# Hybrid encoder block on one Trainium2 core: a new order of the beginning (norm gains spread by TensorE, weight split shared by two engines, idle TensorE fed transposes)

## The chip, the cores and the metric

The kernel runs on one core of one Trainium2 chip. The metric is the time of one execution in device microseconds, the median of three runs. Times of single instructions come from one profiled execution. Engines are named as the profile names them: PE is TensorE, DVE is VectorE, ACT is ScalarE, POOL is GpSimd, SP issues the DMAs.

## The reference, cut to what matters

One layer, 1024 tokens of width 1024, all in float32:

```
h    = rmsnorm(x, norm_mix)                  # x * rsqrt(mean(x*x) + eps) * norm_mix
proj = h @ w_in                              # 2208 columns, split in
qa, ka, va, ga, cq, ckv, kr, gb              # 512,128,128,512,384,256,32,512
ya = window_attention(qa, ka, va) * silu(ga)
q  = rmsnorm(cq, q_a_norm) @ w_uq            # latent attention
kv = rmsnorm(ckv, kv_a_norm) @ w_ukv
yb = latent_attention(q, kv, rope(kr)) * silu(gb)
out = rmsnorm(x + concat(ya, yb) @ w_out, final_norm)
```

The change touches only the start: `h`, and the "natural" part of the projection, the 800 columns `va`, `cq`, `ckv`, `kr`, which come out with the tokens on the partitions.

## The kernel before, in words

Every float32 product is made of three matmuls: each operand is split in a part `hi` rounded to the fp32r type and the rest `lo`, and `three()` adds hi*hi, hi*lo and lo*hi in PSUM (L1097 to L1101). There are eight blocks `k` of 128 weight rows (`KT`) and eight tiles `t` of 128 tokens (`NT`). Each engine runs its own instruction list strictly in the order in which the code issues it, and the engines meet only at semaphores, so the order around the change is written out by hand.

The path of one token tile at the start: SP loads `x_in` (512 KB, two buffers). ACT squares it and sums the row (`s_ssq`). DVE turns the sum into a variance (`s_var`), ACT takes the root (`s_rms`), DVE takes the reciprocal and multiplies x, the scale and the gains `g_mix` in one instruction (L831, `s_xn`). PE transposes the tile in eight pieces into PSUM banks 0 and 1 (`turn_x`, `s_xT`). ACT copies each bank to `hT_hi` (`h_hi`), DVE subtracts it to make `hT_lo` (`h_lo`, `s_hT`). The gains were loaded by a DMA that writes `norm_mix` to all 128 partitions.

The path of one weight block: SP loads 800 of its columns into one of three buffers `wn_raw`. POOL copies them to `wn_hi` (L406) and subtracts for `wn_lo` (L408), then signals `s_wnr`.

PE multiplies tile t with block k by `natural(t, c, ks)`, in two column groups c: 416 columns (va, ckv, kr) in one PSUM bank and 384 (cq) in another, three matmuls each. `nat_banks(t)` gives the banks of tile t; there are three pairs, so tile 3 takes those of tile 0. Tiles 0 to 2 are worked on together, block by block, as blocks come in; the transposes of tiles 3 to 7 are put between the blocks. From tile 3 on, PE does a whole tile at a time, and before each waits for `s_lat` of the tile three before it: ACT and DVE must have taken that tile out of its banks. They do this in the "lat loop" (L613 and L848), whose first step is tile 0 and which both engines enter only after the last `h_hi` and `h_lo`: a copy of va, two squares with sums, a copy of kr, a root, a reciprocal and two scaled writes of `lat` (L861, L864; `s_lat`). `lat` is then transposed (`turn_lat`). Behind this stage come the up-projections and the attention, in which PE goes on without long pauses.

Of the kernel before, what the change touches and what calls it, by code (L numbers as in the profile page):

```python
# [32 lines left out]
P = 128  # L33
# [26 lines left out]
NA = P + KVL + ROPE  # L60
NW = NA + QL

# [9 lines left out]
def encoder(nc, x, norm_mix, w_in, attn_sink, q_a_norm, w_uq, kv_a_norm, w_ukv, w_out, final_norm,  # L72
# [7 lines left out]
    with ExitStack() as ctx:  # L80
# [21 lines left out]
        g_lat = at("g_lat", 144.5, [P, QL + KVL])  # L102
        lat = at("lat", 147, [P, 2, QL + KVL])
# [62 lines left out]
        ssq, var, rms, rstd = (stat[:, 8 * i:8 * i + 8] for i in range(4))  # L166
        lss, lvar, lrms, lrstd = (stat[:, 32 + 2 * i:34 + 2 * i] for i in range(4))
# [20 lines left out]
        s_wnh, s_wnr = sem("wn_hi_ready"), sem("wn_ready")  # L188
        s_pA, s_pB = sem("natA_done"), sem("natB_done")
# [88 lines left out]
        def _(sp):  # L278
            def load_x(t):
                if t >= 2:  # L280
                    sp.wait_ge(s_xn, t - 1)
                sp.dma_start(x_in[:, t % 2, :], x[t * P:(t + 1) * P, :]).then_inc(s_x[t % 2], 16)

            def load_wn(k):
                if k >= 3:
                    sp.wait_ge(s_wnr, k - 2)
                rows = w_in[k * P:(k + 1) * P, :]
                sp.dma_start(wn_raw[:, k % 3, 0:P], rows[:, VA:VA + P]).then_inc(s_wn[k % 3], 16)
                sp.dma_start(wn_raw[:, k % 3, P:NA], rows[:, CKV:CKV + KVL + ROPE]).then_inc(s_wn[k % 3], 16)
                sp.dma_start(wn_raw[:, k % 3, NA:NW], rows[:, CQ:CQ + QL]).then_inc(s_wn[k % 3], 16)  # L290
# [15 lines left out]
            sp.wait_ge(s_wnr, KT)  # L306
# [96 lines left out]
        def _(pool):  # L403
# [176 lines left out]
        def _(act):  # L580
# [10 lines left out]
            for t in range(NT):  # L591
                if t == 3:
                    h_hi(t - 1)
# [19 lines left out]
            for t in range(NT):  # L613
                a, b = nat_banks(t)
                act.wait_ge(s_pA, t + 1)
                nc.scalar.activation(vA[:, t, :, 0:HD], ps[:, a, 0:P].rearrange("p (g c) -> p g c", c=HD),
                                     ACT.Copy)
                if t >= 2:
                    act.wait_ge(s_lT, t - 1)
                nc.scalar.activation(lat[:, t % 2, QL:QL + KVL], ps[:, a, P:P + KVL], ACT.Square,  # L620
                                     accum_out=lss[:, 1:2])
                nc.scalar.activation(kr_n[:, t, :], ps[:, a, P + KVL:NA], ACT.Copy).then_inc(s_va, 1)
                act.wait_ge(s_pB, t + 1)
                nc.scalar.activation(lat[:, t % 2, 0:QL], ps[:, b, 0:QL], ACT.Square,
                                     accum_out=lss[:, 0:1]).then_inc(s_lss, 1)
# [177 lines left out]
        def _(dve):  # L803
# [17 lines left out]
            for t in range(NT):  # L821
                if t == 3:
                    h_lo(t - 1)
                dve.wait_ge(s_ssq, t + 1)
                nc.vector.tensor_scalar(var[:, t:t + 1], ssq[:, t:t + 1], 1.0 / D, EPS, ALU.mult,
                                        ALU.add).then_inc(s_var, 1)
                dve.wait_ge(s_rms, t + 1)
                link(nc.vector.reciprocal(rstd[:, t:t + 1], rms[:, t:t + 1]))
                if t == 0:
                    dve.wait_ge(s_gmix, 16)  # L830
                nc.vector.scalar_tensor_tensor(out=x_n[:, t % 2, :], in0=x_in[:, t % 2, :],  # L831
                                               scalar=rstd[:, t:t + 1], in1=g_mix[:, :], op0=ALU.mult,
                                               op1=ALU.mult).then_inc(s_xn, 1)
                if t >= 1 and t != 3:
                    h_lo(t - 1)
# [12 lines left out]
            for t in range(NT):  # L848
# [247 lines left out]
        def _(pe):  # L1096
# [19 lines left out]
            def natural(t, c, ks):
# [3 lines left out]
                for k in ks:  # L1120
                    last = three(ps[:, nat_banks(t)[c], 0:w1 - w0], hT_hi[:, k, toks], hT_lo[:, k, toks],
# [14 lines left out]

            pe.wait_ge(s_id, 2)

            turn_x(0)
            turn_x(1)  # L1140
            for k in range(KT - 2):
                for t in range(3):
                    if k == 0:
                        pe.wait_ge(s_hT, 2 * (t + 1))
                    pe.wait_ge(s_wnr, k + 1)
                    for c in range(2):
                        natural(t, c, range(k, k + 1))
                    if k == 0 and t == 0:
                        turn_x(2)
                if k >= 1:  # L1150
                    turn_x(2 + k)
            pe.wait_ge(s_wnr, KT)
            for t in range(3):
                for c in range(2):
                    natural(t, c, range(KT - 2, KT))
# [256 lines left out]
```

## Time and profile before

| what | value |
|---|---|
| median of 3 runs | 655.42 us (654.73 to 655.53) |
| the profiled execution's own time | 655.55 us |
| its span in the trace | 653.8 us |
| PE busy | 632.7 us, 97% of the span |
| DVE, ACT, POOL busy | 407.8, 331.8, 302.1 us |

PE's busy time and the span differ by 21.1 us. The page's 40 slices are 16.3 us each: PE has a 3 in the first, a 6 in the last and 9 in all others, so the larger part of PE's idle time lies in the first 20 us.

### The profile page before, as it was taken

How to read it: one execution, taken by the hardware profiler on the slowest of the kernel's cores; microseconds unless marked ns; L12 is line 12 of the kernel's file. 1: busy time of each engine (PE TensorE's matmuls, PEld its weight loads, DVE VectorE, ACT ScalarE, POOL GpSimd, SP SyncE). 2: the span in 40 equal slices, each digit the busy share in tenths (PEclk: the TensorE clock that was granted, in tenths of full speed). 3: DMA queues.
4: the chain of work that ended last, by engine and by line, in shares of the span. 5: the costliest groups of instructions: out<-in, count | busy, mean ns of one | idle time of the engine just before them, and what ended most of it. 6: DMA issues, size and time to landing. Idle time of an engine off the chain costs nothing.

```text
span 653.8 us, 8923 instructions
## 1 busy us (share of the span) xinstructions
PE 632.7 (97%) x3252; PEld 536.6 (82%) x3252; DVE 407.8 (62%) x773; ACT 331.8 (51%) x717; POOL 302.1 (46%) x283
## 2 busy tenths in 40 slices
PE   3999999999999999999999999999999999999996
PEld 3899998888888878888878788888888887888884
DVE  4863326334221158999985988888888888955422
ACT  4542222213222147777774877777777778404312
POOL 4962004402323244363545776876786777820000
PEclk9999999999999999999999999999999999999998
DMA  7730006363121210100122101011013201403521
GB/s 238 232 123 0 1 29 240 142 250 101 34 65 33 64 34 1 32 2 1 48 99 73 40 2 42 12 30 41 1 42 102 100 1 34 161 1 125 181 81 65
DMA packets 31612, 47.38 MB, mean 72 GB/s; under 512 B 2544, under 2 KB 19440, under 8 KB 31440
## 3 DMA queue, kind: packets, MB, share of 16 engines
q1 hardware_dynamic: 31568, 46.81, 22.6%
q8 instruction: 26, 0.43, 0.3%
q14 instruction: 18, 0.15, 0.1%
HBM read 35.13 MB, written 11.67 MB: 72 GB/s over the span
## 4 chain that ended last, share of the span: by engine, by line
PE 91%; DVE 3%; ACT 2%; issue 1%; DMA 1%; POOL 1%; SPq 0%; ACTq 0%; DVEq 0%; POOLq 0%
PE ps L1099 21%; PE ps L1101 21%; PE ps L1100 21%; PE ps L1308 8%; PE ps L1324 4%; PE ps L1325 4%; PE ps L1241 2%; PE ps L1251 2%; PE ps L1252 1%; PE ps L1230 1%; PE ps L1229 1%; DMA g_mix<-norm_mix 1%; PE ps L1111 1%; PE ps L1133 1%; DVE x_n L831 1%
## 5 line engine op out<-in xcount | busy, mean ns | idle before, releaser
L523 POOL TENSOR_SCALAR p_b<-p_b,stat 128x1024 f32<-128x1024 f32 x64 | 71.9, 1123 | 52.9 <-DVE stat L1023 52.2
L738 ACT ACTIVATE pT_hi<-ps 128x512 fp32r<-128x512 f32 x128 | 69.9, 596 | 38.5 <-PE ps L1308 38.4
L1018 DVE TENSOR_REDUCE stat<-ps 128x1 f32<-128x1024 f32 x64 | 77.7, 1213 | 10.2 <-PE ps L1101 10.1
L1099 PE MATMUL ps<-hT_hi,w_hi 128*128 128x512 f32 x208 | 83.7, 402 | 0.0
L1028 DVE TENSOR_TENSOR pT_lo<-ps,pT_hi 128x512 fp32r<-128x512 f32 x128 | 81.8, 680 | 1.4 <-ACT pT_hi L738 1.4
L1101 PE MATMUL ps<-hT_hi,w_lo 128*128 128x512 f32 x208 | 81.3, 391 | 0.0
L1100 PE MATMUL ps<-hT_lo,w_hi 128*128 128x512 f32 x208 | 81.0, 390 | 0.0
L729 ACT ACTIVATE p_b<-ps,stat 128x1024 f32<-128x1024 f32 x64 | 71.5, 1118 | 12.0 <-DVE stat L1018 11.7
L1308 PEld LDWEIGHTS ps<-ident,p_b 128*128 128x128 f32 x512 | 59.3, 141 | 12.1 <-issue 2.6
L1308 PE MATMUL ps<-ident,p_b 128*128 128x128 f32 x512 | 67.3, 273 | 1.0 <-DVE pT_lo L1028 0.9
L406 POOL TENSOR_SCALAR w_hi<-w_raw 128x1024 fp32r<-128x1024 f32 x13 | 14.1, 1081 | 91.4 <-PE ps L1101 91.4
L466 POOL TENSOR_SCALAR p_w<-p_w,stat 128x384 f32<-128x384 f32 (+1 forms) x48 | 27.8, 596 | 60.1 <-DVE stat L949 60.1
L1324 PE MATMUL ps<-pT_hi,vB 128*128 128x512 f32 x128 | 55.3, 432 | 0.0
L1101 PE MATMUL ps<-k_hi,q_lo 96*128 96x512 f32 x128 | 50.5, 394 | 0.0
L1100 PE MATMUL ps<-k_lo,q_hi 96*128 96x512 f32 x128 | 50.5, 394 | 0.0
L1099 PE MATMUL ps<-k_hi,q_hi 96*128 96x512 f32 x128 | 50.3, 393 | 0.0
L1325 PE MATMUL ps<-pT_lo,vB 128*128 128x512 f32 x128 | 50.3, 393 | 0.0
L1101 PE MATMUL ps<-wo_hi,y_lo 128*128 128x512 f32 x128 | 49.8, 389 | 0.0
L1100 PE MATMUL ps<-wo_lo,y_hi 128*128 128x512 f32 x128 | 49.8, 389 | 0.0
L1099 PE MATMUL ps<-wo_hi,y_hi 128*128 128x512 f32 x128 | 49.8, 389 | 0.0
L1099 PE MATMUL ps<-wn_hi,hT_hi 128*128 128x384 f32 (+1 forms) x128 | 45.7, 357 | 0.4 <-DVE hT_lo L815 0.4
L1101 PEld LDWEIGHTS ps<-hT_hi,w_lo 128*128 128x128 f32 x208 | 39.0, 188 | 8.5
(155 smaller groups left out, 1433.1 us busy)
## 6 DMA issues: line engine op xcount, KB each, us to landing
w_raw<-w_in SPq DMA_DIRECT2D x13, 512.0 KB, 3.9
x_in<-x SPq DMA_DIRECT2D x8, 512.0 KB, 3.7
wo_raw<-w_out SPq DMA_DIRECT2D x8, 512.0 KB, 4.4
x_r<-x SPq DMA_DIRECT2D x8, 512.0 KB, 3.7
out<-o_n SPq DMA_DIRECT2D x16, 256.0 KB, 2.4
q_nope_scratch<-stage SPq DMA_DIRECT2D x8, 256.0 KB, 2.8
k_nope_scratch<-stage SPq DMA_DIRECT2D x8, 256.0 KB, 2.1
v_scratch<-stage SPq DMA_DIRECT2D x8, 256.0 KB, 2.0
```

What stands on the lines that cost most here:

```text
L466: nc.gpsimd.tensor_scalar(p_w[:, u % 2, r, 0:w], p_w[:, u % 2, r, 0:w], w_col(5, u)[:, r:r + 1], 0.5, ALU.mult, ALU.mult).then_inc(s_wp, 1)
L523: nc.gpsimd.tensor_scalar(p_b[:, (U + 1) % 4, :], p_b[:, (U + 1) % 4, :], r_b[:, U % 4:U % 4 + 1], 0.5, ALU.mult, ALU.mult).then_inc(s_bp, 1)
L729: nc.scalar.activation(p_b[:, (U + 1) % 4, :], ps[:, b:b + 2, :].rearrange("p b c -> p (b c)"), ACT.Exp, bias=nm_b[:, U % 4:U % 4 + 1], ac ...
L738: nc.scalar.activation(pT_hi[:, G % 2, 4 * a:4 * a + 4, U % 4 * P:(U % 4 + 1) * P], ps[:, 4 + a, :].rearrange("p (k c) -> p k c", c=P), AC ...
L1018: nc.vector.tensor_reduce(nm_b[:, U % 4:U % 4 + 1], ps[:, b:b + 2, :].rearrange("p b c -> p (b c)"), AX.X, ALU.max, negate=True).then_inc( ...
L1028: nc.vector.tensor_tensor(pT_lo[at_], ps[:, 4 + a, :].rearrange("p (k c) -> p k c", c=P), f(pT_hi[at_]), ALU.subtract).then_inc(s_bTl, 1)
L1099: nc.tensor.matmul(o, a_hi, b_hi, start=first, stop=False)
L1100: nc.tensor.matmul(o, a_hi, b_lo, start=False, stop=False)
L1101: return nc.tensor.matmul(o, a_lo, b_hi, start=False, stop=last)
L1308: last = nc.tensor.transpose(ps[:, 4 + a, k * P:(k + 1) * P], p_b[:, (U + 1) % 4, (4 * a + k) * P:(4 * a + k + 1) * P], ident[:, :])
L1324: nc.tensor.matmul(o, vB[:, hp, k, :], pT_hi[:, G % 2, k, :], start=(k == 0), stop=False)
L1325: last = nc.tensor.matmul(o, vB[:, hp, k, :], pT_lo[:, G % 2, k, :], start=False, stop=(k == NT - 1))
```

## The change

The gains come as eight rows of 128 numbers (`g_row`, 4 KB); PE transposes them to a column for each block (`g_col`), and then spreads each column over the partitions by transposing a broadcast of it into banks 6 and 7. Tiles 0 and 1 are scaled from there (`gain = ps[:, 6 + a, :]`), and ACT keeps a copy in `g_mix` for the later tiles (`keep_g`). The row sum of tile 0 is made in halves, one on ACT and one on DVE. All tiles are scaled in halves, each with its own signal. `wn_hi` is made by ACT, and POOL makes only `wn_lo`, in two pieces with a signal each. The column groups are regrouped to va with cq (512 columns) and ckv with kr (288). SP's order and the order of the work on PE, ACT and DVE at the start are new. `spin(n)` issues n transposes of the identity that nothing reads.

```diff
-NA = P + KVL + ROPE
-NW = NA + QL
+NA = P + QL
+NW = NA + KVL + ROPE
...
-            sp.dma_start(g_mix[:, :], norm_mix.partition_broadcast(P)).then_inc(s_gmix, 16)
-            load_x(1)
-            load_wn(0)
+            sp.dma_start(g_row[:, :], norm_mix.rearrange("(k c) -> k c", c=P)).then_inc(s_grow, 16)
+            load_wn(0)
+            load_x(1)
...
             for k in range(KT):
-                pool.wait_ge(s_wn[k % 3], 48 * (k // 3 + 1))
-                split(wn_raw[:, k % 3, :], wn_hi[:, k, :], wn_lo[:, k, :], s_wnh, k + 1, s_wnr)
+                pool.wait_ge(s_wnh, k + 1)
+                for w0, w1 in ((0, NA), (NA, NW)):
+                    nc.gpsimd.tensor_tensor(wn_lo[:, k, w0:w1], wn_raw[:, k % 3, w0:w1], f(wn_hi[:, k, w0:w1]),
+                                            ALU.subtract).then_inc(s_wnr, 1)
...
+            def wn_hi_k(k):
+                act.wait_ge(s_wn[k % 3], 32 * (k // 3 + 1))
+                nc.scalar.activation(wn_hi[:, k, :], wn_raw[:, k % 3, :], ACT.Copy).then_inc(s_wnh, 1)
...
+                    if t < 2:
+                        dve.wait_ge(s_gb, a + 1)
+                        gain = ps[:, 6 + a, :]
...
+            dve.wait_ge(s_gT, 1)
+            nc.vector.tensor_copy(g_col[:, :], ps[:, 3, 0:KT]).then_inc(s_gcol, 1)
+            for t in range(4):
+                norm_x(t)
+                if t < 3:
+                    h_lo(t)
...
+            spin(20)
+            pe.wait_ge(s_grow, 16)
+            nc.tensor.transpose(ps[:, 3, 0:KT], g_row[:, :], ident[0:KT, 0:KT]).then_inc(s_gT, 1)
+            pe.wait_ge(s_gcol, 1)
...
+            turn_x(0)
+            spin(8)
+            both(0, (0,))
+            spin(8)
+            turn_x(1)
+            spin(6)
+            both(0, (1,))
+            both(1, (0, 1))
+            both(0, (2,))
+            both(1, (2,))
+            turn_x(2)
+            both(0, (3,))
+            both(1, (3,))
+            both(2, range(4))
+            turn_x(3)
+            for k in (4, 5):
+                for t in range(3):
+                    both(t, (k,))
+                turn_x(k)
+            both(0, (6, 7))
+            turn_x(6)
+            both(1, (6, 7))
+            both(2, (6, 7))
+            turn_x(7)
             for t in range(3, NT):
                 pe.wait_ge(s_hT, 2 * (t + 1))
                 pe.wait_ge(s_lat, t - 2)
```

`both(t, ks)` is `natural` for both column groups. The orders that the prediction speaks of, as the built programs have them, follow; the name before `<-` is what is written, and the words in brackets are the semaphores waited for.

PE at its start, before. The transposes of tiles 0 and 1 stand first, and the first matmuls behind them.

```order
L1111 MATMUL ps<-ident,x_n 128x128 [waits xn_ready,ident_ready]
L1111 MATMUL ps<-ident,x_n 128x128 x7
L1111 MATMUL ps<-ident,x_n 128x128 [waits hT_ready,xn_ready]
L1111 MATMUL ps<-ident,x_n 128x128 x3
L1111 MATMUL ps<-ident,x_n 128x128 [waits hT_ready]
L1111 MATMUL ps<-ident,x_n 128x128 x3
L1099 MATMUL ps<-wn_hi,hT_hi 128x416 [waits wn_ready,hT_ready]
```

PE at its start, now.

```order
L1218 MATMUL ps<-ident 128x128 [waits ident_ready]
L1218 MATMUL ps<-ident 128x128 x19
L1223 MATMUL ps<-ident,g_row 128x8 [waits g_row_in]
L1227 MATMUL ps<-ident,g_col 128x128 [waits g_col_ready]
L1227 MATMUL ps<-ident,g_col 128x128 x7
L1178 MATMUL ps<-ident,x_n 128x128 [waits xn_ready]
L1178 MATMUL ps<-ident,x_n 128x128 x3
L1178 MATMUL ps<-ident,x_n 128x128 [waits xn_ready]
```

Twenty unread transposes and the nine that spread the gains moved ahead of tile 0.

ACT behind the root of tile 0, before: the square of tile 1 stands directly behind that root.

```order
L600 ACTIVATE stat<-stat 128x1 [waits var_ready]
L597 ACTIVATE x_n,stat<-x_in 128x1024 [waits x_in1]
L600 ACTIVATE stat<-stat 128x1 [waits var_ready]
L584 ACTIVATE hT_hi<-ps 128x4x128 [waits xT_done] x2
L597 ACTIVATE x_n,stat<-x_in 128x1024 [waits xT_done,x_in0]
```

The same place now.

```order
L614 ACTIVATE stat<-stat 128x1 [waits var_ready]
L618 ACTIVATE wn_hi<-wn_raw 128x800 [waits wn_in0]
L596 ACTIVATE hT_hi<-ps 128x4x128 [waits xT_done] x2
L611 ACTIVATE x_n,stat<-x_in 128x1024 [waits x_in1]
L614 ACTIVATE stat<-stat 128x1 [waits var_ready]
L618 ACTIVATE wn_hi<-wn_raw 128x800 [waits wn_in1]
L622 ACTIVATE g_mix<-ps 128x512 [waits xn_ready] x2
L596 ACTIVATE hT_hi<-ps 128x4x128 [waits xT_done] x2
```

Tile 1's square moved behind tile 0's copies, and ACT makes `wn_hi` and keeps `g_mix` between them.

PE where tile 3 begins. Before, the last matmuls of tile 2 stand directly ahead of tile 3's, and `turn_x(7)` lies thirty-six matmuls further up.

```order
L1099 MATMUL ps<-wn_hi,hT_hi 128x384
L1100 MATMUL ps<-wn_lo,hT_hi 128x384
L1101 MATMUL ps<-wn_hi,hT_lo 128x384
L1099 MATMUL ps<-wn_hi,hT_hi 128x416 [waits lat_ready,hT_ready]
L1100 MATMUL ps<-wn_lo,hT_hi 128x416
```

The same place now.

```order
L1167 MATMUL ps<-wn_lo,hT_hi 128x288
L1168 MATMUL ps<-wn_hi,hT_lo 128x288
L1178 MATMUL ps<-ident,x_n 128x128 [waits hT_ready,xn_ready]
L1178 MATMUL ps<-ident,x_n 128x128 x3
L1178 MATMUL ps<-ident,x_n 128x128 [waits hT_ready,xn_ready]
L1178 MATMUL ps<-ident,x_n 128x128 x3
L1166 MATMUL ps<-wn_hi,hT_hi 128x512 [waits lat_ready,hT_ready]
```

The transposes of tile 7 moved to directly ahead of tile 3.

## Rows read from the trace of the kernel before

**Rows 1.** The page, part 1: busy time of each engine

```profile
PE 632.7 (97%) x3252; PEld 536.6 (82%) x3252; DVE 407.8 (62%) x773; ACT 331.8 (51%) x717; POOL 302.1 (46%) x283
```

**Rows 2.** Windows of PE: length, busy (count), granted clock, DMA share, GB/s

```profile
8.00:9.94 1.94, 1.94 (x8) 1.00 1.06 380
11.68:15.60 3.92, 3.92 (x14) 1.00 0.56 132
17.32:19.57 2.25, 2.25 (x14) 1.00 1.00 318
19.96:48.51 28.55, 28.55 (x173) 1.00 0.51 165
```

**Rows 3.** The chain of waits, pieces: start, length, what

```profile
1.17 5.29 DMA g_mix<-norm_mix
...
13.63 2.94 DVE x_n L831
...
24.61 0.87 PE ps L1111 x8
...
95.97 0.23 PE ps L1100
```

**Rows 4.** Timeline of PE: start, length, instruction, idle before it

```profile
19.96 0.46 PE L1099 MATMUL ps<-wn_hi,hT_hi 128*128 128x416 f32 x1 [0.39 <-DVE hT_lo L815]
...
48.51 0.35 PE L1099 MATMUL ps<-wn_hi,hT_hi 128*128 128x416 f32 x1
```

**Rows 5.** Timeline of ACT, first tile

```profile
4.13 1.06 ACT L597 ACTIVATE x_n<-x_in 128x1024 f32<-128x1024 f32 x1 [1.90 <-DMA x_in<-x]
...
5.50 0.20 ACT L600 ACTIVATE stat<-stat 128x1 f32<-128x1 f32 x1 [0.22 <-DVE stat L825]
```

**Rows 6.** Timeline of DVE, first tile

```profile
5.32 0.15 DVE L825 TENSOR_SCALAR stat<-stat 128x1 f32<-128x1 f32 x1 [5.32 <-ACT x_n L597]
5.74 0.16 DVE L828 RECIPROCAL stat<-stat 128x1 f32<-128x1 f32 x1 [0.27 <-ACT stat L600]
...
10.85 1.28 DVE L815 TENSOR_TENSOR hT_lo<-ps,hT_hi 128x512 fp32r<-128x512 f32 x2
```

**Rows 7.** Timeline of POOL, first two weight blocks

```profile
9.84 2.85 POOL L408 TENSOR_TENSOR wn_lo<-wn_raw,wn_hi 128x800 fp32r<-128x800 f32 x1
...
13.59 1.90 POOL L408 TENSOR_TENSOR wn_lo<-wn_raw,wn_hi 128x800 fp32r<-128x800 f32 x1
```

**Rows 8.** Timeline from turn_x(7) to the end of tile 0's lat, PE, ACT and DVE

```profile
41.08 1.04 PE L1111 MATMUL ps<-ident,x_n 128*128 128x128 f32 x8
41.71 1.09 ACT L584 ACTIVATE hT_hi<-ps 128x512 fp32r<-128x512 f32 x2 [3.07 <-PE ps L1111]
...
43.29 0.28 ACT L616 ACTIVATE vA<-ps 128x128 fp32r<-128x128 f32 x1 [0.49 <-PE ps L1101]
...
43.46 0.38 ACT L620 ACTIVATE lat<-ps 128x256 f32<-128x256 f32 x1
...
44.33 0.49 ACT L624 ACTIVATE lat<-ps 128x384 f32<-128x384 f32 x1 [0.32 <-PE ps L1101]
...
44.72 0.20 ACT L624 ACTIVATION_READ_ACCUMULATOR lat<-ps 128x1 f32 x1
...
45.20 0.20 ACT L629 ACTIVATE stat<-stat 128x2 f32<-128x2 f32 x1 [0.28 <-DVE stat L855]
...
45.63 0.62 DVE L861 SCALAR_TENSOR_TENSOR lat<-ps,stat,g_lat 128x384 f32<-128x384 f32 x1
...
46.17 0.48 DVE L864 SCALAR_TENSOR_TENSOR lat<-ps,stat,g_lat 128x256 f32<-128x256 f32 x1
```

**Rows 9.** Groups with shapes apart: busy, mean ns of one

```profile
L436 POOL TENSOR_TENSOR uq_lo<-uq_raw,uq_hi 128x512 fp32r<-128x512 f32 x3 | 3.9, 1291 | 0.1
```

**Rows 10.** One line, L934: its tensor_tensor_reduce, duration min/median/max

```profile
L934 DVE CUSTOM_DVE_ANT_0 p_w<-distb,ps,nsink x64: 470/609/617, 232.9 to 339.4; 128x384 f32<-128x384 f32 x48, 128x256 f32<-128x256 f32 x16
```

More of the change, by code:

```diff
@@ L102, in encoder @@
         g_lat = at("g_lat", 144.5, [P, QL + KVL])
+        g_row = at("g_row", 201, [KT, P])
+        g_col = at("g_col", 204, [P, KT])
         lat = at("lat", 147, [P, 2, QL + KVL])
@@ L590, in _, with square_x @@
             nc.scalar.activation(oss[:, 0:1], ident[:, 0:1], ACT.Sqrt)
-            for t in range(NT):
-                if t == 3:
-                    h_hi(t - 1)
+            def square_x(t):
                 act.wait_ge(s_x[t % 2], 16 * (t // 2 + 1))
@@ L818, in h_lo, with norm_x @@
                                             ALU.subtract).then_inc(s_hT, 1)
[L821 to L826, printed above, removed]
+            def norm_x(t):
+                if t == 0:
+                    dve.wait_ge(s_x[0], 16)
+                    link(nc.vector.tensor_tensor_reduce(out=x_n[:, 0, HALF:], in0=x_in[:, 0, HALF:],
+                                                        in1=x_in[:, 0, HALF:], scale=1.0 / D, scalar=EPS,
+                                                        op0=ALU.mult, op1=ALU.add, accum_out=sq_b))
+                    dve.wait_ge(s_ssq, 1)
+                    nc.vector.tensor_tensor(var[:, 0:1], ssq[:, 0:1], sq_b, ALU.add).then_inc(s_var, 1)
+                else:
+                    dve.wait_ge(s_ssq, t + 1)
+                    nc.vector.tensor_scalar(var[:, t:t + 1], ssq[:, t:t + 1], 1.0 / D, EPS, ALU.mult,
+                                            ALU.add).then_inc(s_var, 1)
@@ L827, in _ @@
                 dve.wait_ge(s_rms, t + 1)
                 link(nc.vector.reciprocal(rstd[:, t:t + 1], rms[:, t:t + 1]))
[L829 to L835, printed above, removed]
+                for a in range(2):
+                    cols = slice(a * HALF, (a + 1) * HALF)
+                    if t < 2:
+                        dve.wait_ge(s_gb, a + 1)
+                        gain = ps[:, 6 + a, :]
+                    else:
+                        dve.wait_ge(s_gmix, a + 1)
+                        gain = g_mix[:, cols]
+                    nc.vector.scalar_tensor_tensor(out=x_n[:, t % 2, cols], in0=x_in[:, t % 2, cols],
+                                                   scalar=rstd[:, t:t + 1], in1=gain, op0=ALU.mult,
+                                                   op1=ALU.mult).then_inc(s_xn, 1)
@@ L836, in _ @@
+            dve.wait_ge(s_gT, 1)
[4 more added lines that the diff above has]
+                    h_lo(t)
+            for t in range(4, NT):
+                norm_x(t)
+                h_lo(t - 1)
             h_lo(NT - 1)
@@ L860, in _ @@
                 link(nc.vector.reciprocal(lrstd, lrms))
-                nc.vector.scalar_tensor_tensor(out=lat[:, t % 2, 0:QL], in0=ps[:, b, 0:QL],
+                nc.vector.scalar_tensor_tensor(out=lat[:, t % 2, 0:QL], in0=ps[:, a, P:NA],
                                                scalar=lrstd[:, 0:1], in1=g_lat[:, 0:QL], op0=ALU.mult,
                                                op1=ALU.mult)
-                nc.vector.scalar_tensor_tensor(out=lat[:, t % 2, QL:QL + KVL], in0=ps[:, a, P:P + KVL],
+                nc.vector.scalar_tensor_tensor(out=lat[:, t % 2, QL:QL + KVL], in0=ps[:, b, 0:KVL],
                                                scalar=lrstd[:, 1:2], in1=g_lat[:, QL:QL + KVL],
@@ L1120, in natural @@
                 for k in ks:
+                    if t < 3 and c == 0 and k in (0, 4):
+                        pe.wait_ge(s_hT, 2 * t + 1 + k // 4)
+                    if t == 0 or (t == 1 and k < 3):
+                        pe.wait_ge(s_wnr, 2 * k + c + 1)
+                    if t == 2 and c == 0 and k == 0:
+                        pe.wait_ge(s_gmix, 2)
                     last = three(ps[:, nat_banks(t)[c], 0:w1 - w0], hT_hi[:, k, toks], hT_lo[:, k, toks],
@@ L1135, in turn_lat, with both, spin @@
                 last.then_inc(s_lT, 1)
[L1137 to L1145, printed above, removed]
+            def both(t, ks):
+                for k in ks:
                     for c in range(2):
                         natural(t, c, range(k, k + 1))
[L1148 to L1155, printed above, removed]
+            def spin(n):
+                for _ in range(n):
+                    nc.tensor.transpose(ps[:, 4, 0:P], ident[:, :], ident[:, :])
+            pe.wait_ge(s_id, 2)
+            spin(20)
+            pe.wait_ge(s_grow, 16)
+            nc.tensor.transpose(ps[:, 3, 0:KT], g_row[:, :], ident[0:KT, 0:KT]).then_inc(s_gT, 1)
+            pe.wait_ge(s_gcol, 1)
+            for a in range(2):
+                for k in range(4):
+                    last = nc.tensor.transpose(ps[:, 6 + a, k * P:(k + 1) * P],
+                                               g_col[:, 4 * a + k:4 * a + k + 1].to_broadcast([P, P]), ident[:, :])
+                last.then_inc(s_gb, 1)
+            turn_x(0)
[22 more added lines that the diff above has]
+            turn_x(7)
             for t in range(3, NT):
```

79 lines of the change are left out of this document (59 added, 20 removed).

## The prediction

> **What bounds the kernel now.** The page first: PE is busy for 97% of the span [rows 1]. Then windows of PE alone: from 19.96 us to 48.51 us it has no idle time [rows 2], and 48.51 is where tile 3 begins, with no wait before it [rows 4]. So behind 19.96 a microsecond is saved only if PE starts its unbroken run earlier or if the run stays unbroken. Before 19.96 PE did three `turn_x` and two block-tile pairs (a pair is six matmuls). The window from 11.68 holds eight transposes and one pair in 3.92 us, the one from 17.32 the same 14 instructions in 2.25 us [rows 2]. The clock column says 1.00 for both, but the work of the first goes at half the rate of the second, 1.2 against 2.4 GHz. PE had been idle until 8.00 and in pauses up to 11.68, had run from there to 15.60, and ran at the full rate from 17.32.
>
> What held PE up stands in the chain of waits: the DMA of the gains (issued at 1.17, 5.29 us), and tile 2's scaling, which took 2.94 us from 13.63 [rows 3] where 1024 elements need about 1.28 (two 512 pieces of L815 [rows 6]). POOL's L408 had begun at 13.59 and took 1.90 [rows 7]: DVE stood still until it ended. The Trainium skill (SBUF — State Buffer, "Who interferes with whom") says that a DVE instruction with two SBUF inputs and a reading GpSimd instruction exclude each other for the whole instruction. This trace agrees.
>
> **The change: how early the run starts.** I work the new order through; an instruction costs its row.
> - Spins. The identity is ready at about 1.5 us (POOL's first instructions; an estimate). Eight transposes at half rate take 1.94 with the last one's drain [rows 2], so 0.22 each: spin(20) ends at 6.0 if all go at half rate, at 5.0 if the clock rises halfway. I take 6.0. The gains' 4 KB row is the second DMA; even at 6.46, when the 512 KB one landed [rows 3], it would cost 0.5.
> - Gains and tile 0. Transpose of `g_row` and its drain 0.3, DVE copy 0.15: 6.4. The half sum on DVE stands behind that copy, though x landed at 4.13 [rows 5]: the nearest row is 0.61 for 384 elements [rows 10], so 0.75 for 512, plus 0.1 to read the sum: 7.2. Sum, root, reciprocal 0.15 + 0.20 + 0.16 with three handovers of 0.03 [rows 5, 6]: 7.8. Two scaled halves of 0.75 (0.62 for 384 in L861 [rows 8]): 8.6 and 9.3. Before, the whole tile was scaled at 7.86, so the first product is not earlier; the spread gains buy only what the spins take back. `turn_x(0)`, now at the full rate, 0.87 for eight [rows 3]; from a bank's first transpose to `hT_hi` 0.63 (41.08 to 41.71), and two copies end 1.09 later [rows 8]: about 10.5.
> - Tile 1. Its square stands behind those copies: 10.5 + 1.06 + 0.20 = 11.7; sum, root, reciprocal: 12.3; halves at 13.0 and 13.7; bank 0 transposed at 13.7, bank 1 at 14.4. ACT keeps the gains (2 x 0.55) until 14.3, then `hT_hi` 14.9, `hT_lo` 15.6. Beside it: `wn_hi(1)` (800 elements, 0.85 by the 1.06 for 1024 [rows 5]) until 12.9, POOL's pieces 1.29 [rows 9] and about 0.8: 14.2 and 15.0. PE: spin(6) until 14.8, pair (0, 1) until 15.9, then the pair of tile 1, block 0, at **16.0**.
>
> These halves read the gains from PSUM. By the rule on shared inputs above they don't stand still beside POOL. The nearest row agrees: L815, one PSUM input, took 1.28 for two from 10.85 while POOL ran its 9.84 instruction until 12.69 [rows 6, 7]. If they stood still after all, it would be one POOL piece, 1.3 later.
>
> From there the run is unbroken. PE needs 3.3 us for a block in three tiles (28.55 less five times 0.87, over 22 pairs, is 1.1 a pair), POOL 2.1 for its two pieces. Tile 2 is transposed when PE comes to it (20.4): its square ends near 17.5, its halves, beside one POOL piece, near 20. That and `wn_lo(3)` near 22 are the tight places, with 0.3 to 0.5 us to spare; later tiles have over 1.
>
> The run holds 22 pairs and five `turn_x`, from (1, 0) to `turn_x(7)`; from 19.96 to 48.51 the old one held 22 pairs and five `turn_x` too, in 28.55 us [rows 2]. The new widths cost nothing: 0.23 for 512 columns [rows 3], 0.19 for 416 (24 matmuls of it in 4.53 us from 48.51), a slope by which 288 cost 0.13, together what 416 and 384 cost; a weight load is no more than 0.11, as transposes follow at that pace [rows 3]. So `turn_x(7)` starts at 16.0 + 28.55 = **44.55**, where before everything up to tile 3 ended at 48.51. On this count the start gains 4.0 - 0.9 for the transposes of tile 7 = 3.1 us.
>
> **The change: where tile 3 begins.** `turn_x(7)` now stands directly ahead of tile 3, which waits for tile 0's `lat`. ACT and DVE take up the lat loop only after the last `h_hi` and `h_lo`, those of tile 7. Before, `turn_x(7)` ran at 41.08 with 7.4 us of matmuls behind it, and `lat` of tile 0 was written at 46.65, 1.9 us before PE wanted it [rows 4, 8]. Now nothing covers this chain: from the first transpose to `hT_hi` 0.63; two copies 1.06 until the next can start; copy of va 0.17 (43.29 to 43.46); square of 384 with its sum 0.59 (44.33 to 44.92); copy of kr 0.10 (at most the 0.20 of the smallest ACT row); square of 256 with its sum 0.48 (0.38, less the 0.10 by which a sum overlaps its square, and 0.20); two small DVE operations 0.24; root 0.24; reciprocal 0.20; two writes 1.02 (45.63 to 46.65); back to PE 0.04: **4.8 us** from the start of `turn_x(7)` [rows 5, 6, 8]. PE fills 0.9 of it with the transposes and is idle for 3.9.
>
> **The sum.** Tile 3 begins at 44.55 + 4.8 = 49.35, plus 0.1 for a first matmul after a pause (0.46 against 0.35 [rows 4]), 49.45 against 48.51: 0.95 later. Behind it the same work: tiles 3 to 7 still have 8 us each for the 3 us of their lat chain. The profiled execution took 655.55 in all (span 653.8), 0.13 over the median of 655.42; the 0.95 is added to the median: **656.4 us**. All the edits of the start gain 3.1, and one edit of the order gives back 3.9 and 0.1.
>
> **The rivals.**
> - The pause makes the clock fall. 3.9 us without a matmul is more than any pause of PE behind 17.32, and longer than the two of 1.7 before it (9.94 to 11.68, 15.60 to 17.32). PE would then run at half rate for about as long as from 11.68 to 15.60 [rows 2]: 3.92 us with half lost, 2.0 more, 658.4. The longest pauses seen before say nothing for it, since the rate was low in them anyway. The Trainium skill (TensorE: Matmul & The Clock Gate, Part 1) has the clock fall after a stretch of idleness, and rise with activity: the rule speaks for the spins and against this pause.
> - The clock stays low through the spins, until past 12 us. The spread gains then come at 8.4, tile 1 a microsecond later and the first pairs at half rate: the run starts 1.5 to 2.5 later, 658.4. Against it: it rose after 3.92 us of nearly unbroken work, and spin(20) alone is 4.4.
> - The other side: the pause behind `turn_x(7)` isn't there, because tile 0's lat is ready before. Then tile 3 begins at 45.5 and the time is 652.4. It takes ACT entering the lat loop before tile 7's copies, against the order. With the pause in place the start alone decides: the kernel is no slower if the run begins by 15.0, and measurably faster if it begins by 13.7.
>
> **How the numbers follow.** A measurement of this kernel tells 0.2%, 1.3 us, from no change. The main case, chance 0.65: 656.4, own range 655.2 to 657.6 (start between 14.9, if the clock rises within spin(20) and handovers are short, and 17.1, with the 1.3 for POOL). Fallen clock 0.12, low clock at the start 0.10, no pause 0.13. The main case lies above 656.7 for 0.2 of its 0.65, so slower is 0.42, same 0.45, faster 0.13. Range: 655.0 to 658.6 leaves out the fast case and a little at either end.
>
> **What would show it.** The chain of waits has no DMA of the gains; `g_col` is written near 6.4; PE's (1, 0) starts near 16.0; `turn_x(7)` near 44.5, followed by an idle PE for 3.9 us, released by DVE's second `lat` write; the first matmuls of tile 3 at 0.23 apart (0.44 if the clock fell). I am wrong if PE's idle time there is under 2 us, or if (1, 0) starts before 14.5 or after 17.5.

## The result, and the profile after

The changed kernel takes 657.88 us in the median of five runs (657.08 to 658.87); the kernel before took 655.53 (654.73 to 656.27) on the same chip. The ratio is 1.0036, with a 95% interval 1.0021 to 1.0051: slower by a little over a third of a per cent. The profiled execution took 657.08, the shortest of the five, with a span (first to last instruction in the trace) of 655.3 against 653.8.

The page of the changed kernel, part 1, answers to [rows 1]:

```profile
PE 639.4 (98%) x3303; PEld 534.9 (82%) x3303; DVE 405.8 (62%) x784; ACT 337.6 (52%) x727; POOL 292.1 (45%) x283
```

The waits of PE, the longest first (total, times, longest):

```profile
PE ps L1166 <- DVE lat L931: 3.9, 1, 3.9
PE ps L1218 <- POOL ident L425: 1.5, 1, 1.5
PE ps L1178 <- DVE x_n L890: 0.9, 1, 0.9
```

PE is busier by 6.7 us, of which 51 instructions more (the unread transposes and the spreading) are a part, and one wait stands out: tile 3's first matmul for the `lat` of tile 0. The timeline of PE shows the start and that place:

```profile
1.52 3.78 PE L1218 MATMUL ps<-ident 128*128 128x128 f32 x20 [1.52 <-POOL ident L425]
5.71 1.09 PE L1227 MATMUL ps<-ident,g_col 128*128 128x128 f32 x8 [0.26 <-DVE g_col L895]
7.73 1.31 PE L1178 MATMUL ps<-ident,x_n 128*128 128x128 f32 x8 [0.93 <-DVE x_n L890]
...
15.08 0.39 PE L1166 MATMUL ps<-wn_hi,hT_hi 128*128 128x512 f32 x1
...
43.47 1.04 PE L1178 MATMUL ps<-ident,x_n 128*128 128x128 f32 x8
48.38 0.47 PE L1166 MATMUL ps<-wn_hi,hT_hi 128*128 128x512 f32 x1 [3.88 <-DVE lat L931]
48.69 0.56 PE L1167 MATMUL ps<-wn_lo,hT_hi 128*128 128x512 f32 x1
...
49.47 0.63 PE L1166 MATMUL ps<-wn_hi,hT_hi 128*128 128x512 f32 x1
49.90 0.63 PE L1167 MATMUL ps<-wn_lo,hT_hi 128*128 128x512 f32 x1
...
52.34 0.40 PE L1167 MATMUL ps<-wn_lo,hT_hi 128*128 128x512 f32 x1
52.57 0.40 PE L1168 MATMUL ps<-wn_hi,hT_lo 128*128 128x512 f32 x1
```

The run begins with pair (1, 0) at 15.08 and comes to `turn_x(7)` at 43.47. Then PE is idle for 3.88 us, and tile 3 starts at 48.38, where before it started at 48.51 [rows 4]: the whole gain of the start is gone, to 0.13 us. And then most matmuls follow each other at 0.43 us instead of 0.23, until 52.03. Windows of PE (length, busy, granted clock, DMA share, GB/s) say the same, against [rows 2]:

```profile
15.08:43.47 28.39, 28.39 (x175) 1.00 0.62 197
44.40:48.38 3.98, 0.10 (x2) 1.00 0.01 2
48.38:52.23 3.85, 3.85 (x10) 0.56 0.00 0
52.23:55.75 3.52, 3.52 (x18) 1.00 0.00 0
```

TensorE's clock was at its upper level, 2.4 GHz, in the run, and at the lower one, 1.2 GHz, for most of the 3.85 us behind the pause (0.56 is the mean of both). Ten steps from 48.38 to 52.34 took 3.96 us; at full rate they are 0.31 + 9 x 0.23 = 2.38: **1.6 us** lost. The span grew by 1.5 = 1.6 - 0.13.

What PE waited for, on ACT and DVE, against [rows 8]:

```profile
44.10 1.08 ACT L596 ACTIVATE hT_hi<-ps 128x512 fp32r<-128x512 f32 x2 [4.14 <-PE ps L1178]
45.07 0.28 ACT L663 ACTIVATE vA<-ps 128x128 fp32r<-128x128 f32 x1
45.23 0.51 ACT L667 ACTIVATE lat<-ps 128x384 f32<-128x384 f32 x1
...
46.79 0.20 ACT L676 ACTIVATE stat<-stat 128x2 f32<-128x2 f32 x1 [0.51 <-DVE stat L922]
...
47.76 0.47 DVE L931 SCALAR_TENSOR_TENSOR lat<-ps,stat,g_lat 128x256 f32<-128x256 f32 x1
```

The chain is the one foretold: two copies of tile 7, then the lat loop, whose last write for tile 0 ends at 48.23.

### The profile page after: what moved, and what is told of

Read it like the earlier page. It is cut to its first block, busy times and chain, and to the rows that moved or that the text cites. A ratio compares the mean times of both kernels' runs of the same rounds, so it can differ in the third digit from the quotient of the medians.

```text
span 655.3 us, 9053 instructions
## 1 busy us (share of the span) xinstructions
PE 639.4 (98%) x3303; PEld 534.9 (82%) x3303; DVE 405.8 (62%) x784; ACT 337.6 (52%) x727; POOL 292.1 (45%) x283
## 4 chain that ended last, share of the span: by engine, by line
PE 92%; DVE 3%; ACT 2%; issue 2%; POOL 1%; POOLq 0%; ACTq 0%
PE ps L1166 21%; PE ps L1168 21%; PE ps L1167 21%; PE ps L1407 8%; PE ps L1423 4%; PE ps L1424 4%; PE ps L1340 2%; PE ps L1350 2%; PE ps L1351 1%; PE ps L1329 1%; PE ps L1328 1%; PE ps L1178 1%; PE ps L1218 1%; PE ps L1206 1%; POOL p_w L478 1%
## 5 line engine op out<-in xcount | busy, mean ns | idle before, releaser
L1085 DVE TENSOR_REDUCE stat<-ps 128x1 f32<-128x1024 f32 x64 | 77.6, 1213 | 10.2 <-PE ps L1168 10.1
L1166 PE MATMUL ps<-wn_hi,hT_hi 128*128 128x288 f32 (+1 forms) x128 | 45.7, 357 | 3.9 <-DVE lat L931 3.9
```

The source lines that it names most:

```text
L1085: nc.vector.tensor_reduce(nm_b[:, U % 4:U % 4 + 1], ps[:, b:b + 2, :].rearrange("p b c -> p (b c)"), AX.X, ALU.max, negate=True).then_inc( ...
L1166: nc.tensor.matmul(o, a_hi, b_hi, start=first, stop=False)
```

## The experiments

Each was timed in five rounds or more beside the kernel before, whose median lay between 655.5 and 656.3. Experiments 1 to 4 share a chip, and so do 5, 8, 9 and 10, then 6 and 11, then 7 and 12; across these groups the ratios to the kernel before compare better than the times.

**1. lat0_first: the pause taken away.** ACT and DVE do tile 0's step of the lat loop before tile 7's copies.

```diff
-            h_hi(7)
             for t in range(NT):
+                if t == 1:
+                    h_hi(7)
```

The same for `h_lo(7)` on DVE.

> The changed kernel, with ACT and DVE taking tile 0's lat ahead of tile 7's two copies and subtractions; PE's order is untouched. Theory (pause and clock): tile 3's start waits for tile 0's lat only because that stands behind tile 7's copies. Then lat of tile 0 is written near 42, PE goes from turn_x(7) straight into tile 3 at about 44.4 us at the full rate, and both the 3.9 us pause and the 1.9 us of nine slow matmuls are gone: 657.9 - 5.8 = 652.1 us, 3.4 below the kernel before. Rival (the loss is at the start, in spins and ACT's added work, and the pause covers another wait): the pause shrinks but a later one takes its place, and the time stays at 655.5 or above.

Measured: 651.86 us, ratio 0.9937 [0.9923, 0.9950]. Timeline of DVE and PE:

```profile
42.42 0.47 DVE L933 SCALAR_TENSOR_TENSOR lat<-ps,stat,g_lat 128x256 f32<-128x256 f32 x1
...
43.36 1.04 PE L1180 MATMUL ps<-ident,x_n 128*128 128x128 f32 x8
...
44.15 0.47 PE L1168 MATMUL ps<-wn_hi,hT_hi 128*128 128x512 f32 x1
44.46 0.39 PE L1169 MATMUL ps<-wn_lo,hT_hi 128*128 128x512 f32 x1
```

`lat` is written at 42.89, PE doesn't stop, and the steps are 0.23 from the second on. By the medians 6.0 us less than the changed kernel, with nothing else touched. By the spans of the profiled executions it is 5.8: 4.2 for the earlier start of tile 3 (48.38 - 44.15), which is the pause and a little more, and 1.6 for the clock.

**2. turn7_up: the pause made shorter.** `turn_x(7)` stands ahead of tile 2's last two pairs.

```diff
-            both(2, (6, 7))
             turn_x(7)
+            both(2, (6, 7))
```

> The changed kernel with turn_x(7) moved ahead of the pairs of tile 2 with blocks 6 and 7, which cover 2.2 us of the lat chain. Theory: tile 3 would be reached at 44.4, tile 0's lat is written 4.8 us after turn_x(7) starts at 41.3, so near 46.1: a pause of 1.7 us, as short as those before 17 us in the kernel before, and no fall of the clock. 657.9 - 2.2 - 1.9 = 653.8 us. If only the pause counts and the slow matmuls come anyway: 655.7. Rival (loss at the start): no change from 657.9.

Measured: 653.66 us, ratio 0.9965 [0.9953, 0.9978]. The pause is 1.71 us:

```profile
46.47 0.47 PE L1166 MATMUL ps<-wn_hi,hT_hi 128*128 128x512 f32 x1 [1.71 <-DVE lat L931]
46.78 0.39 PE L1167 MATMUL ps<-wn_lo,hT_hi 128*128 128x512 f32 x1
47.01 0.40 PE L1168 MATMUL ps<-wn_hi,hT_lo 128*128 128x512 f32 x1
```

The clock held: the steps are 0.23 from the second on.

**3. fed_pause: the wait kept, the idleness taken away.** Behind `turn_x(7)` PE waits for its `hT_lo` and then makes 20 transposes that nothing reads.

```diff
             turn_x(7)
+            pe.wait_ge(s_hT, 2 * NT)
+            for _ in range(20):
+                nc.tensor.transpose(ps[:, 0, 0:P], ident[:, :], ident[:, :])
```

> The changed kernel with 20 more unread transposes of the identity in the pause, from when tile 7's hT is complete (46.0 us) on: they take 2.2 us and end before tile 0's lat is there, so tile 3 still begins at 48.4. Theory: PE's idle time is cut to 1.6 us in one piece, the clock stays at the full rate, the nine matmuls that took 0.43 us each take 0.23: 657.9 - 1.8 = 656.1 us. Rival (the first matmuls of tile 3 are slow for another reason, such as banks or operands just written): they stay at 0.43 apart and the time at 657.9.

Measured: 656.17 us, ratio 1.0003 [0.9994, 1.0012].

```profile
44.20 1.04 PE L1178 MATMUL ps<-ident,x_n 128*128 128x128 f32 x8
46.81 2.40 PE L1257 MATMUL ps<-ident 128*128 128x128 f32 x20 [1.57 <-DVE hT_lo L862]
49.12 0.47 PE L1166 MATMUL ps<-wn_hi,hT_hi 128*128 128x512 f32 x1
49.42 0.39 PE L1167 MATMUL ps<-wn_lo,hT_hi 128*128 128x512 f32 x1
```

Tile 3 starts 0.74 later than in the changed kernel and the span is 0.8 shorter: that is the clock's price alone, 1.5 us. Such work doesn't shorten the wait, but takes the second cost off it.

**4. pause_on_before: the pause put into the kernel before.** One thing moved there, `turn_x(7)` to directly ahead of tile 3.

```diff
-                if k >= 1:
+                if 1 <= k < 5:
...
+            turn_x(7)
```

> The kernel before, with turn_x(7) alone moved to directly ahead of tile 3, nothing else changed. Theory: the transposes start at 47.6, tile 0's lat is written 4.8 us later, tile 3 begins at 52.4 instead of 48.5, 3.9 later; with the fall of the clock another 1.9: 655.5 + 5.8 = 661.3 us (659.4 if the clock holds). Rival (the order of the end matters only together with the new start): within 1 us of 655.5.

Measured: 660.80 us, ratio 1.0069 [1.0057, 1.0082]. PE's timeline, and two windows behind the pause:

```profile
46.67 1.04 PE L1111 MATMUL ps<-ident,x_n 128*128 128x128 f32 x8
51.35 0.42 PE L1099 MATMUL ps<-wn_hi,hT_hi 128*128 128x416 f32 x1 [3.65 <-DVE lat L864]
51.62 0.35 PE L1100 MATMUL ps<-wn_lo,hT_hi 128*128 128x416 f32 x1
51.80 0.35 PE L1101 MATMUL ps<-wn_hi,hT_lo 128*128 128x416 f32 x1
...
52.61 0.55 PE L1101 MATMUL ps<-wn_hi,hT_lo 128*128 128x416 f32 x1
```

```profile
52.30:56.20 3.90, 3.90 (x15) 0.59 0.02 4
56.30:60.00 3.70, 3.70 (x25) 1.00 0.00 0
```

The one move costs 5.1 us by the medians (655.67 and 660.80) without any other edit of the change, and the clock falls here too, a few matmuls after work is taken up. By the spans it is only 4.4, because this execution came to `turn_x(7)` about 1.0 sooner than the old start would have it (46.67, where 48.51 less 0.79 for the transposes is 47.72); the section on the prediction says why. The six kernels side by side; the last column is the span less the start of tile 3, that is, how long the same work behind it took:

| kernel | pause | tile 3 at | span | rest |
|---|---|---|---|---|
| before [rows 4] | none | 48.51 | 653.8 | 605.3 |
| lat0_first | none | 44.15 | 649.5 | 605.3 |
| turn7_up | 1.71 | 46.47 | 651.9 | 605.4 |
| fed_pause | 1.57, then fed | 49.12 | 654.5 | 605.4 |
| changed kernel | 3.88 | 48.38 | 655.3 | 606.9 |
| pause_on_before | 3.65 | 51.35 | 658.2 | 606.9 |

Two groups, 1.5 us apart: where PE was idle for 3.65 us or more ahead of tile 3 the rest took 606.9, where for 1.71 or less 605.3 or 605.4. In all six PE had worked for over 20 us with hardly a gap before it came to this place. At the start, where it had not, the clock fell behind shorter pauses too (experiments 9 and 10), so the two groups give no length of a pause that is safe everywhere.

**5. no_spins.** lat0_first without all 42 unread transposes (`for _ in range(0)`).

> The version without the pause (tile 0's lat ahead of tile 7's copies, 651.9 us), with all 42 unread transposes left out. The clock theory: PE's first own work then goes at half rate. The gains are spread about 0.5 us sooner, but 16 transposes of tiles 0 and 1 and the first two or three pairs take twice as long; the unbroken run starts at 16 to 17 us instead of 15: 653.4 us, 1 to 2 above. Rival (the gain of the start comes from the order and the spread gains, the spins only fill idle time): within 0.5 us of 651.9.

Measured: 651.33 us, ratio 0.9935 [0.9922, 0.9947], where 653.4 was expected. The expectation missed, and the rival that it named, within 0.5 us of 651.9, came nearly true:

```profile
4.21 0.24 PE L1225 MATMUL ps<-ident,g_row 8*128 8x8 f32 x1 [4.21 <-DMA g_row<-norm_mix]
4.72 1.97 PE L1229 MATMUL ps<-ident,g_col 128*128 128x128 f32 x8 [0.26 <-DVE g_col L896]
6.75 1.97 PE L1180 MATMUL ps<-ident,x_n 128*128 128x128 f32 x8
```

The gains' row lands at 4.21, but spin(20) keeps PE until 5.2. Without it PE works at half rate until about 14.0, and yet pair (1, 0) starts at 14.96, against 15.03 in lat0_first. The long spin costs as much as the faster clock gives.

**6. spin12.** lat0_first with `spin(12)` in place of `spin(20)`, so that it ends when the row lands.

> lat0_first with twelve unread transposes instead of twenty ahead of the gains' transpose; the other unread transposes stay. They start at 1.52 and end near 4.2 at 0.22 each, when the gains' row lands (4.21 in no_spins), so they hold up nothing. Theory (the long spin delays the gains by what the faster clock gives back): g_col at 4.5 and x_n(0) at 5.95 as in no_spins, and the clock rises during the spreading or turn_x(0), so that everything up to pair (1, 0) comes 0.8 to 1.0 us sooner than with twenty: pair (1, 0) near 14.2, time 651.0 or less. Rival (the pauses around the small steps keep the clock low until turn_x(1) without the long spin): pair (1, 0) near 15.0 and 651.3 to 651.9, as with twenty or none.

Measured: 650.58 us (650.42 to 651.35), ratio 0.9923 [0.9909, 0.9936]. Pair (1, 0) at 14.17, as expected:

```profile
1.53 2.82 PE L1220 MATMUL ps<-ident 128*128 128x128 f32 x12 [1.53 <-POOL ident L425]
...
4.81 1.18 PE L1229 MATMUL ps<-ident,g_col 128*128 128x128 f32 x8 [0.26 <-DVE g_col L896]
6.82 1.31 PE L1180 MATMUL ps<-ident,x_n 128*128 128x128 f32 x8 [0.84 <-DVE x_n L891]
```

This is the lowest median of all versions: 5 us under the kernel before, 7 under the changed one. Against lat0_first and no_spins the intervals of the ratios touch or overlap; what shows the gain is the earlier start of pair (1, 0), by 0.8 to 0.9.

**7. whole_x.** spin12, both halves of a scaled tile signalled behind the second.

```diff
-                                                   op1=ALU.mult).then_inc(s_xn, 1)
+                                                   op1=ALU.mult)
+                    if a == 1:
+                        ins.then_inc(s_xn, 2)
```

> spin12, but both halves of a scaled tile are signalled together, behind the second, so that a tile is in effect scaled whole; nothing else changes. Theory (the handover in halves is a large part of what the start gains): turn_x(0) and turn_x(1) each start 0.66 later (one half is 0.70 by two halves in 1.41, and PE needs 0.04 to take it up), both on the chain to pair (1, 0): 1.2 to 1.4 later, near 15.5, and the time 651.8 to 652.1 by spin12's 650.58. Rival (PE's own work between the tiles covers it): pair (1, 0) within 0.3 of 14.17 and the time within 0.4 of spin12's.

Measured: 652.72 us, ratio 0.9940 [0.9928, 0.9953]; beside spin12's ratio that is 0.17% or 1.1 us more, by the spans 1.5 (650.1 against 648.6). Pair (1, 0) starts at 15.30, 1.13 later. The profiled execution of whole_x also spread the gains at a lower rate (1.96 us, in spin12 1.18), but so did that of keep_late (experiment 12, 1.91), which hands over in halves, differs from spin12 otherwise only in ACT's two copies, and starts pair (1, 0) at 14.25. So the handover in halves is worth 1.1 to 1.5 us of what the start gains, by traces with the same rate 1.05.

**8. gain_by_dma.** lat0_first with `g_mix` loaded by the old DMA, the spreading and `keep_g` left out, and `spin(29)`.

> The version without the pause (651.9 us), with the gains written to all partitions by the DMA of before; tiles 0 and 1 are scaled from SBUF, ACT keeps no copy, and 29 unread transposes stand where 20 and the nine spreading ones stood. My reading of the prediction (the spread gains buy only what spins and transposes take back): the scaling of tile 0 starts at 6.5 instead of 6.9, the first weights and x of tile 1 land 1 to 2 us later but are wanted only at 6.6 and 9.6, and DVE may stand still beside POOL in tile 1: 651.9 to 653.2, taken as 652.3. Rival (the 512 KB DMA was what held the start up, as the chain of waits of before has it): 1.5 to 2.5 above, 653.9.

Measured: 652.39 us, ratio 0.9952 [0.9938, 0.9965]: 0.5 above lat0_first by the medians, 1.1 by the spans (650.6 against 649.5), with overlapping intervals. What costs this is not when the gains arrive. Tile 0's scaling starts sooner than in lat0_first, at 6.44 against 6.87. But POOL's first piece of `wn_lo` comes later, at 8.58 instead of 7.49, and tile 1's halves, now with the gains in SBUF, take 2.43 us beside POOL instead of 1.41. DVE's timeline:

```profile
11.30 2.43 DVE L885 SCALAR_TENSOR_TENSOR x_n<-x_in,stat,g_mix 128x512 f32<-128x512 f32 x2
```

Pair (1, 0) starts at 16.04, against 15.03. Behind spin(20) the spread gains are worth 0.5 to 1.1 us, through where they are read from and through the weights, not through an earlier tile 0.

**9. spins_on_before.** The kernel before with 36 unread transposes ahead of `turn_x(0)` and 8 behind it.

> The kernel before, with 36 unread transposes ahead of tile 0's and 8 between tile 0's and tile 1's. The clock is then up from about 5 us on, so the first transposes and the first pair take 2 us less. Theory: what sets the run's start at 19.96 is tile 2's scaling on DVE (13.63 to 16.57) behind x's DMA and POOL's port, which no faster PE moves: within 0.4 us of 655.6. Rival (half rate itself cost the time): 1 to 2 us less.

Measured: 656.35 us (653.78 to 657.35, 12 runs), ratio 1.0002 [0.9989, 1.0014]. No change in the time that can be told. But the faster start that it was meant to test wasn't there for long: the clock was up by 7.69, where `turn_x(0)` takes 1.09 us, then PE waits 1.91 us for `hT_lo`, and behind this wait the clock falls. A window of PE over the first pair of tile 0:

```profile
12.25:15.50 3.25, 3.16 (x12) 0.50 0.50 131
```

The pair goes at half rate, as in the kernel before. So the result doesn't settle what a full rate up to the run would bring there.

**10. hi_on_pool.** lat0_first with `wn_hi` made by POOL, as before.

> The version without the pause (651.9 us), with wn_hi made by POOL again (ACT's eight copies left out; wn_lo still in two pieces). POOL needs 0.9 + 2.0 us a block plus DVE's turns at the shared port, about 3.5; PE uses a block in three tiles in 3.3 and starts with two blocks in hand. Theory (POOL's pace no longer counts once tiles 0 and 1 come early): wn_lo(3) is ready near 19.5 when PE wants it at 20.3: within 0.5 us of 651.9. Rival (POOL is the second bound): PE waits for blocks 3 and later, 1.5 us or more above, 653.4 to 655.

Measured: 653.10 us (651.28 to 654.90, 11 runs), ratio 0.9963 [0.9950, 0.9975]: 1.2 above lat0_first where 0.5 at most was expected. PE waits for no block in its trace; what is late is the start, and one line of DVE's timeline beside POOL's shows 0.5 of it:

```profile
6.42 1.04 POOL L430 TENSOR_SCALAR wn_hi<-wn_raw 128x800 fp32r<-128x800 f32 x1 [4.95 <-DMA wn_raw<-w_in]
...
6.79 0.68 DVE L871 TENSOR_TENSOR stat<-stat 128x1 f32<-128x1 f32 x1
```

DVE's sum of two numbers, 0.16 us in the changed kernel, ended when POOL's instruction ended, with root, reciprocal and both halves behind it. This execution's spin(20) had also taken 0.54 longer (4.26 against 3.72), so `turn_x(0)` starts 1.06 later than in lat0_first (8.74 against 7.68). PE had then waited 1.45 us, and the clock fell. A window of PE:

```profile
8.75:12.00 3.25, 3.25 (x16) 0.51 0.55 179
```

`turn_x(0)` and spin(8) go at half rate, pair (0, 0) starts at 12.05 instead of 9.75, and pair (1, 0) at 16.79 instead of 15.03. These 1.76 us are the difference of the spans (651.3 and 649.5). The spread of its runs, 3.6 us, is wide, and one trace doesn't show how often this happens.

**11. sum_first.** spin12 with DVE's half sum ahead of the copy to `g_col`.

> spin12 with DVE's half sum of tile 0 ahead of the copy to g_col, instead of behind it. x lands at 4.0, so the sum can start 0.5 us sooner, at 4.05, and ends at 4.8; the copy follows at 4.8 instead of 4.5, and the spreading with it. Theory: ACT's half (4.02 to 4.74) is then ready together with it, x_n(0) could come at 5.5, but its gains are spread only by 4.9 + 1.0 (first bank, half rate) = 5.9: 0 to 0.1 us sooner than spin12, time within 0.3 of it. Rival (DVE's order was the limit): 0.4 us sooner throughout.

Measured: 651.33 us (650.25 to 651.71), ratio 0.9930 [0.9917, 0.9942]: no gain, 0.75 more in the median, intervals overlapping. Neither the theory (within 0.3 of spin12) nor the rival (0.4 sooner) came out. The sum did start sooner, at 4.11, but the spreading waited for the copy until 5.07, and in the profiled execution PE went at half rate until about 10.2.

**12. keep_late.** spin12 with ACT's two copies to `g_mix` behind tile 1's `hT_hi`.

> spin12, but ACT copies the gains to g_mix (two copies, 1.25 us) behind tile 1's two hT_hi copies instead of ahead of them; everything else stays. Theory (ACT's copies are on the chain of tile 1): PE has transposed bank 0 of tile 1 near 11.9 and ACT comes to it at 12.40; with the copies behind, hT_hi starts near 11.9, so pair (1, 0) comes up to 0.5 sooner, near 13.7, and the time is 650.1. Rival (POOL's wn_lo(1), which PE needs for pair (0, 1), lands no sooner, or PE's own work fills the time): pair (1, 0) within 0.15 of 14.17, time within 0.3 of 650.58.

Measured: 650.90 us (650.88 to 651.00), ratio 0.9918 [0.9904, 0.9931]: the same as spin12. ACT came to `hT_hi` at 12.04 instead of 12.40, but pair (1, 0) started at 14.25: PE's spin(6) and pair (0, 1) stand ahead of it anyway. The rival held.

## Why the prediction was right in sign and short in size

**What bounds the kernel.** Right: all six spans of the table are the start of tile 3 plus the same rest, but for the 1.5 to 1.6 us of the clock.

**Spins.** "I take 6.0" was wrong by 0.8: spin(20) ended near 5.2. The clock rose within it (20 transposes in 3.78 us instead of 4.4), which I had only as the lower end. It carried through unchanged: `x_n(0)` at 6.92 instead of 7.8, tile 1's halves from 11.37 instead of 12.3, pair (1, 0) at 15.08 instead of 16.0.

**"The spread gains buy only what the spins take back."** Right for tile 0 of the changed kernel, and experiments 5 and 6 show it as a cause: without spins its scaling starts at 5.95, spin(20) puts this off to 6.92, and spin(12) starts it at 6.02 and keeps the faster clock (14.17 for pair (1, 0)). "Only" was too strong: experiment 8 shows that the gains in PSUM also keep tile 1's halves from standing still, 1.0 us.

**Halves that read PSUM don't stand still beside POOL.** Right. Timelines of DVE and of POOL, changed kernel:

```profile
11.37 1.41 DVE L890 SCALAR_TENSOR_TENSOR x_n<-x_in,stat,ps 128x512 f32<-128x512 f32 x2
...
16.84 2.70 DVE L890 SCALAR_TENSOR_TENSOR x_n<-x_in,stat,g_mix 128x512 f32<-128x512 f32 x2
```

```profile
11.98 2.04 POOL L431 TENSOR_TENSOR wn_lo<-wn_raw,wn_hi 128x512 fp32r<-128x512 f32 x2 [2.41 <-ACT wn_hi L618]
15.22 2.07 POOL L431 TENSOR_TENSOR wn_lo<-wn_raw,wn_hi 128x512 fp32r<-128x512 f32 x2 [1.21 <-ACT wn_hi L618]
```

POOL's pair begins while the two halves from PSUM run, and they still take 1.41 us; tile 2's, with the gains in SBUF, take 2.70. The Trainium skill (SBUF — State Buffer, "Who interferes with whom") has a DVE instruction with two inputs in SBUF contend with a GpSimd instruction that reads SBUF, and one with at most one such input, outside DVE's 2-port modes, not. The trace agrees. The tight places held: PE waited neither for tile 2 nor for `wn_lo(3)`.

**The run and the pause.** Right: 28.39 us for the run (28.55 foretold), idle 3.88 (3.9), from the start of `turn_x(7)` to tile 3 4.91 (4.8 and 0.1).

**The clock in the pause.** This is the step that failed. The main case had tile 3 at the full rate, and I gave the fall a chance of 0.12, saying that the longest pauses seen before "say nothing for it", though none of them was as long. Experiments 2, 3 and 4 show that the fall belongs to the pause: shortened or filled, it is gone; put into the kernel before, it is there. Its price was 1.5 to 1.6 us, where the rival had 2.0: of the ten steps behind the pause the first two (0.31 and 0.35 us) and the last (0.31) weren't at half rate yet or any more. The Trainium skill (TensorE: Matmul & The Clock Gate, Part 1) has the clock fall after idleness; ahead of tile 3 it fell behind the pauses of 3.65 and 3.88 us and held through those of 1.57 and 1.71, and I should have weighed that rule as the likelier case.

**The sum.** From the 656.5 that the profiled execution should have taken (656.4 and the 0.13 between it and the median): 1.08 less for the start of `turn_x(7)` (43.47, not 44.55), and 1.6 more for the clock: 657.0, and 657.08 was measured. Two errors of opposite sign left the number close and the range good, while the main case's own range (to 657.6) was missed. That it came out near was in part luck. That the median lies 0.8 above this execution stays open; the last section has a likely source.

**Where the start gains.** By lat0_first 4.4 us in the traces (44.15 against 48.51) and 3.8 by the medians, where 3.1 were foretold. The 4.4 lean on one execution of the kernel before, and its start varies. With the same order up to there, but for unread transposes in the second, pause_on_before begins the run at 17.80 and spins_on_before at 18.03, not at 19.96. In both DVE took up tile 2's scaling ahead of POOL's L408; in the kernel's own trace it came 0.04 later than L408 and stood still for it. DVE and POOL in pause_on_before:

```profile
12.90 1.51 DVE L831 SCALAR_TENSOR_TENSOR x_n<-x_in,stat,g_mix 128x1024 f32<-128x1024 f32 x1
...
13.43 2.75 POOL L408 TENSOR_TENSOR wn_lo<-wn_raw,wn_hi 128x800 fp32r<-128x800 f32 x1
```

Half of that lead was lost again further on (PE waits 0.53 at 22.97), and against this start lat0_first gains 3.3 (44.15 against 46.67 + 0.79). So the standstill of 2.94 us in the prediction's chain is a matter of which engine comes first, and an execution can be without it. Of the 3.8, 1.1 to 1.5 are the halves (experiment 7) and 0.5 to 1.1 the spread gains with their spins (8). No experiment splits the remainder, some 1.2 to 2.2 us. The windows bear on it: before, PE was idle for 1.74, 1.72 and 0.39 us between `turn_x(0)` and the run [rows 2, 4] and worked at half rate until 15.60, while in no_spins it worked at half rate nearly as long but hardly waited. So it is likely the new order of ACT, DVE and PE, and not the clock, that carries it; this is argued from the traces, not shown.

## What to carry to other kernels

When work of one tile is moved to directly ahead of a wait, follow what stands behind its copies on the other engines: here the last two copies were ahead of the whole lat loop, and one line's place in ACT's and DVE's lists was worth 6 us, more than all the edits of the start together (3.8). Price a pause of TensorE twice, once for its length and once for the clock behind it; if the pause must stay, unread transposes take away the second. Don't take a short pause for safe: at the start of these kernels the clock also fell behind 1.91 and 1.45 us. Unread transposes at a start paid only up to the moment at which the data landed: 12 of them started pair (1, 0) 0.8 us sooner than none, 20 of them no sooner.

## What the runs showed of the hardware that I had not expected

- The moment at which the clock rises varies between executions of the same work. Five kernels begin with the same 20 transposes at 1.52 or 1.53; they took 3.72, 3.78, 4.04, 4.26 and 4.53 us (lat0_first, changed kernel, turn7_up, hi_on_pool, fed_pause), and what follows shifts with it: fed_pause comes to `turn_x(7)` 0.73 later than the changed kernel. Three kernels share spin(12) and the spreading, which took 1.18, 1.91 and 1.96 us (spin12, keep_late, whole_x). Such a shift of up to 0.8 us is a likely source of the spread of the runs, and of differences under a microsecond between experiments 6, 11 and 12; no run tests this.
- The lower clock doesn't set in with the first matmul behind a pause. In pause_on_before three follow at 0.18 to 0.27 us, and those from 52.27 at about 0.35. The granted clock reads 1.00 through the whole pause, in the changed kernel until 48.75 and in pause_on_before until past 52.0, and then 0.50.
- The length of the pause alone doesn't decide. The clock held through 1.71 and 1.57 us behind more than 20 us of matmuls with no gap (experiments 2 and 3), and fell behind 1.91 and 1.45 us at the start, where PE had worked for some 8 and 6 us with small gaps (experiments 9 and 10).
- Until the clock has first risen, the windows give a granted clock of 1.00 although PE goes at half rate: the kernel before reads 1.00 from 12.25 to 15.50, where its matmuls go at the pace at which spins_on_before reads 0.50. Once it has risen and fallen, they show the fall, in the first 16 us too. At a start the pace of the matmuls has to be read instead.
- A DVE instruction on one number for each partition, with both inputs in SBUF, stood still beside POOL like a wide one, by the one case in the traces: 0.68 us instead of 0.16 (experiment 10).
